# The Hyena projection inside the first MLP stage of a two-layer diffusion backbone

## The chip, the cores and the metric

The kernel runs on one core of one Trainium2 chip. The metric is the device time of the core in microseconds, as the median over several executions. The engines are TensorE (PE; its weight loads are PEld), VectorE (DVE), ScalarE (ACT), GpSimd (POOL) and SyncE (SP), which in this kernel only issues DMAs.

## The reference

A stream of 1024 latent tokens and one of 256 context tokens, each of width 1024, pass through two layers. Every sub-layer is: RMS norm, shift and scale by the conditioning, the sub-layer, RMS norm, gate, residual. Layer 0 mixes by attention, layer 1 by a Hyena long convolution beside a Mamba-2 scan; both end with a squared-ReLU MLP of hidden width 4096. What matters for the change, cut from the reference:

```python
x = x + mx[5] * rms_norm(sq_relu_mlp(modulate(rms_norm(x, g[2]), mx[3], mx[4]), ff_w1[i], ff_w2[i]), g[3])   # layer 0; ctx likewise
hx = modulate(rms_norm(x, g[0]), mx[0], mx[1])          # layer 1
px = hx @ w_in
hy_x, z_x, m_x = split_cols(px, (ODD_HY, ODD_Z, ODD_XBC + ODD_DT))   # 1536, 512, 1024 + 16 columns
uc = centred_dwconv(hy_x, short_w, short_b)             # 3 taps along the tokens, latent tokens only
m_c = (hc @ w_in[:, ODD_CTX_START:])                    # context tokens: only mamba's columns

z = concatenate([t, cos(ph), -sin(ph)])                 # 33 position features of 1024 positions
h = sin(fr * (z @ w1 + b1))                             # 64 hidden units
h = sin(fr * (h @ w2 + b2))
h = (h @ w3) * decay                                    # the long filters, further on
```

## The kernel before

Features lie on the 128 partitions, tokens along the free axis. The 1280 tokens are worked in three chunks (`CHUNKS`): latent 0 to 511, latent 512 to 1023, and the 256 context tokens. Each float32 product is three products of rounded parts: high by high, high by low and low by high. So every weight piece of 128 x 1024 (512 KB) is fetched by SP, rounded by ACT (`w_high`) and split by DVE (`w_low`, raw less high) before PE uses it; the activations lie likewise as `h_high` and `h_low`. Every engine's instructions are written out in a fixed order, semaphores tie them together, and each function below is a stage: it ends with a barrier of all engines, and its memory and semaphores are new.

`out_and_mlp` (L1181) runs twice, once at the end of each layer. Its work is a list of `steps`, one weight piece each: 24 of the output projection, then for each chunk eight rounds of four pieces up (L1397) and four down (L1414), 216 steps in layer 0. In step i, ACT first rounds piece i+2 and DVE splits piece i+2, SP fetches piece i+3, PE multiplies piece i, and DVE adds the down products to the residual tile (`mixed`, L1602). Six PSUM banks go round. Beside the steps, a table of step numbers (`gate_at`, `square_x_at`, `scale_at` and others, filled in the loop over the six jobs q) places each chunk's closing norm: squares on ACT (L1453), their sum on POOL (L1614), the column sum by an all-ones matmul (L1366), reciprocal root on ACT (L1457, L1459), gating and residual on DVE (L1542, L1551), then the same again for layer 1's opening norm (L1495, L1633, L1372), scale (L1560), shift and rounding (L1503) and splitting (L1535). For the first chunks this lies beside the steps of the next chunk. The last job, q = 5, is the context chunk's; it has no steps left beside it, and the stage runs on without products until `END`.

`project_hyena` (L2293) is the next stage. A `WeightRing` (L334) does fetch, rounding and splitting with two slots; twelve pieces give two units of 512 tokens each, 24 matmuls a unit (L370). ACT copies them to `hy_raw` (L2361), DVE convolves with three operations (L2415 to L2419), SP stores each result to `scratch_hyena`. Beside it the feature network runs: its two small products on PE (L2339), the angle and its reduction to less than half a turn in seven DVE operations a layer (L2377 to L2391), the sine on ACT (L2365), and at the end seven small reversed or shifted copies of the result (`flip`, L2396 to L2403).

`project_mamba` (L1638) follows. It fetches the step-size weights and multiplies them (L1681), then eight xbc pieces of three units each, whose convolution (L1779 to L1783) and SiLU (L1666) lie beside the products, and last four z pieces, two units of 512 each, whose SiLU is the gate (L1737). On DVE only two splits lie beside the z products. The next stage, `scan_states`, opens with 60 transposes on PE (L1823) that ACT copies out (L1831).

## Time and profile before

| | |
|---|---|
| median of three runs | 3692.05 us (3689.9 to 3698.3) |
| profiled execution | 3690.47 us |
| its span | 3688.5 us |
| PE busy | 3471.0 us, 94% |
| DVE, ACT, POOL busy | 1830.5, 1332.2, 690.2 us |
| mean DMA rate | 111 GB/s |

The span runs from the first to the last instruction of the profiled execution; some 2 us lie around it. PE's busy time counts pipelined matmuls whose modelled durations overlap, so the distance from one start to the next says more than the duration. The granted clock (PEclk) has two levels here, 1.00 for 2.4 GHz and 0.50 for 1.2 GHz; a figure between them is a window in which it changed. A line such as L370 is a helper's, shared by several stages, so the place in time has to be given with it.

### The profile page before, as it was taken

To read this page: it belongs to the slowest core of one execution; us is meant where nothing else is said; L and a number is where in the kernel's file an instruction comes from. 1 tells how busy PE (TensorE), PEld (TensorE's weight loads), DVE (VectorE), ACT (ScalarE), POOL (GpSimd) and SP (SyncE) were. 2 spreads that over 40 slices of the span, in tenths; PEclk is the share of its full clock that TensorE was granted. 3 is DMA by queue.
4 is the path that set the end of the run, shared out by engine and by line. 5 is a ranking of instruction groups with operands and counts; after the bars stand their busy time and mean duration, and the time that the engine had idled before them with its cause. 6 is when DMAs were issued, how large, how long until landed. Compare 5 with 4: busy or idle time off the path is not lost. (4 is left out here: it accounts for less than half of the span.)

```text
span 3688.5 us, 40136 instructions
## 1 busy us (share of the span) xinstructions
PE 3471.0 (94%) x15670; PEld 2471.0 (67%) x15670; DVE 1830.5 (50%) x2317; ACT 1332.2 (36%) x2143; POOL 690.2 (19%) x398
## 2 busy tenths in 40 slices
PE   6989799999899999999996989899989899999997
PEld 3655244555688888888886868653344688888886
DVE  3332744433266554554675534476355565444444
ACT  4323344444554333333453223441110443223332
POOL 0000277666332201200211000110000230002001
PEclk8999799999999999999998999998999999999999
DMA  8744532321244333433453211101501343333332
GB/s 336 277 165 122 146 68 58 79 56 45 92 149 136 116 97 97 137 97 97 155 190 126 92 53 40 36 35 58 199 18 52 114 166 97 97 97 120 120 97 97
DMA packets 140528, 408.65 MB, mean 111 GB/s; under 512 B 24621, under 2 KB 41421, under 8 KB 136052
## 3 DMA queue, kind: packets, MB, share of 16 engines
q1 hardware_dynamic: 140340, 406.08, 33.8%
q8 instruction: 125, 2.05, 0.2%
q14 instruction: 63, 0.52, 0.0%
HBM read 344.73 MB, written 61.21 MB: 110 GB/s over the span
## 5 line engine op out<-in xcount | busy, mean ns | idle before, releaser
L1438 ACT ACTIVATE w_high<-w_raw 128x1024 fp32r<-128x1024 f32 x360 | 380.1, 1056 | 579.8 <-PE psum L1414 471.9
L1524 DVE TENSOR_TENSOR w_low<-w_raw,w_high 128x1024 fp32r<-128x1024 f32 x360 | 453.2, 1259 | 119.8 <-ACT w_high L1438 118.8
L1414 PE MATMUL psum<-hid_high,w_high 128*128 128x512 f32 (+1 forms) x1280 | 472.6, 369 | 10.3 <-DVE hid_low L1592 8.7
L1397 PE MATMUL psum<-h_high,w_high 128*128 128x512 f32 (+1 forms) x1280 | 474.7, 371 | 2.1 <-DVE w_low L1524 2.1
L1397 PE MATMUL psum<-h_high,w_low 128*128 128x512 f32 (+1 forms) x1280 | 470.9, 368 | 0.0
L1397 PE MATMUL psum<-h_low,w_high 128*128 128x512 f32 (+1 forms) x1280 | 470.9, 368 | 0.0
L1414 PE MATMUL psum<-hid_low,w_high 128*128 128x512 f32 (+1 forms) x1280 | 470.8, 368 | 0.0
L1414 PE MATMUL psum<-hid_high,w_low 128*128 128x512 f32 (+1 forms) x1280 | 470.8, 368 | 0.0
L1614 POOL TENSOR_TENSOR squares_then_rstd_of_out<-squares_then_rstd_of_out,square_out 128x512 f32<-128x512 f32 (+1 forms) x70 | 102.4, 1464 | 1284.7 <-ACT square_out L1453 1284.1
L1178 POOL TENSOR_TENSOR probs_added<-probs_added,probs_turned 128x1024 f32<-128x1024 f32 x128 | 305.0, 2383 | 66.7 <-ACT probs_turned L1107 62.5
L1146 DVE TENSOR_REDUCE row_max<-psum 128x1 f32<-128x1280 f32 x128 | 190.3, 1491 | 243.6 <-PE psum L1055 147.3
L1589 DVE TENSOR_TENSOR hid_high<-hid_relu 128x512 fp32r<-128x512 f32 (+1 forms) x160 | 113.8, 711 | 350.2 <-ACT hid_relu L1514 350.0
L1107 ACT ACTIVATE probs_turned<-psum 128x512 f32<-128x512 f32 (+1 forms) x352 | 193.5, 577 | 251.5 <-PE psum L1017 249.8
L1414 PEld LDWEIGHTS psum<-hid_high,w_high 128*128 128x128 f32 x1280 | 241.2, 188 | 53.0 <-DVE hid_low L1592 5.8
L370 PE MATMUL psum<-h_high,w_high 128*128 128x512 f32 (+1 forms) x664 | 252.3, 380 | 24.1 <-DVE w_low L363 24.1
L1397 PEld LDWEIGHTS psum<-h_high,w_high 128*128 128x128 f32 x1280 | 241.3, 189 | 44.7 <-DVE w_low L1524 2.7
L1397 PEld LDWEIGHTS psum<-h_low,w_high 128*128 128x128 f32 x1280 | 241.3, 189 | 41.6 <-issue 1.9
L1414 PEld LDWEIGHTS psum<-hid_low,w_high 128*128 128x128 f32 x1280 | 241.3, 188 | 40.1 <-issue 0.2
L1397 PEld LDWEIGHTS psum<-h_high,w_low 128*128 128x128 f32 x1280 | 241.3, 189 | 39.9
L1414 PEld LDWEIGHTS psum<-hid_high,w_low 128*128 128x128 f32 x1280 | 241.3, 189 | 39.8
L370 PE MATMUL psum<-h_low,w_high 128*128 128x512 f32 (+1 forms) x664 | 245.7, 370 | 0.0
L370 PE MATMUL psum<-h_high,w_low 128*128 128x512 f32 (+1 forms) x664 | 245.6, 370 | 0.0
(406 smaller groups left out, 5385.8 us busy)
## 6 DMA issues: line engine op xcount, KB each, us to landing
w_raw<-in_ff_w_dram SPq DMA_DIRECT2D x320, 512.0 KB, 3.5
ada_ring<-in_ada_w_dram SPq DMA_DIRECT2D x24, 2048.0 KB, 9.5
w_raw<-in_w_out_dram SPq DMA_DIRECT2D x40, 512.0 KB, 3.5
stream_in<-scratch_x SPq DMA_DIRECT2D x32, 256.0 KB, 4.0
scratch_spectra<-spectrum_out SPq DMA_DIRECT2D x32, 256.0 KB, 2.0
filter_ring<-scratch_spectra SPq DMA_DIRECT2D x16, 512.0 KB, 4.8
w_raw<-in_w_hy_dram SPq DMA_DIRECT2D x12, 512.0 KB, 3.5
scratch_hyena<-hy_conv SPq DMA_DIRECT2D x12, 512.0 KB
```

The costliest lines, as they stand in the source:

```text
L370: mm = pe.matmul(out, x[:, k, :], y[:, k, a:a + n], start=(k == 0 and i == 0), stop=(k == KT - 1 and i == 2))
L1107: act.activation(pt[:, i % RING, h, 0:nq], g.ps[:, T_BANK + h, 0:nq], ACT.Exp).then_inc(exped, 1)
L1146: dve.tensor_reduce(neg_max[:, u % 2, 4 * h + t:4 * h + t + 1], area[:, 0:TOK], AX.X, ALU.max, negate=True).then_inc(maxed, 1)
L1178: pool.tensor_tensor(total, old, pt[:, i % RING, :, 0:nq], ALU.add).then_inc(added, 1)
L1397: mm = pe.matmul(bank[:, 0:n], x[:, i % SLOTS, k, :], y[:, k, a:a + n], start=(k == 0 and m == 0), stop=(k == KT - 1 and m == 2))
L1414: mm = pe.matmul(bank[:, 0:n], x[:, i % SLOTS, 2 * k + half, :], y[:, k, 0:n], start=(k == 0 and m == 0), stop=(k == HT - 1 and m == 2))
L1438: act.activation(w_hi[:, i % SLOTS], raw[:, i % 2], ACT.Copy).then_inc(w_rounded, 1)
L1524: dve.tensor_tensor(w_lo[:, i % SLOTS], raw[:, i % 2], w_hi[:, i % SLOTS], ALU.subtract).then_inc(w_split, 1)
L1589: dve.tensor_tensor(hid_hi[:, j, 0:n], relu[:, v % 2, 0:n], relu[:, v % 2, 0:n], ALU.mult).then_inc(hid_rounded, 1)
L1614: pool.tensor_tensor(acc_out[:, q % 2, 0:n], acc_out[:, q % 2, 0:n], sq_out[:, v % 2, 0:n], ALU.add).then_inc(added_out, 1)
```

## The change

`project_hyena` is gone. Its twelve weight pieces are steps 216 to 227 of `out_and_mlp` in layer 0 (kind "next"), with that stage's three weight slots and six banks, and the convolution takes its place in DVE's step. The raw products lie in the tile of the MLP's ReLU and square, the results in two rows of the residual tile, from where they are stored. The last job's norm is placed beside these steps, two feature rows a step for gate and residual, four a step for scaling. The convolution no longer pads: it starts with the middle tap over all 1024 tokens and adds the outer two over 1023. The feature network moves into `project_mamba`: its products follow z units 1 and 5, its DVE operations the splits beside z tiles 1 and 3, its sines the gates of units 3 and 7, and `flip` is DVE's last work there. It borrows the raw and accumulator tiles of mamba's convolution, so the positions are fetched once the seventh convolution is done.

```diff
-def out_and_mlp(nc, g, src, w_out, w_ff, x_from, x_mid, x_to, layer, norm_to, tokens):
+def out_and_mlp(nc, g, src, w_out, w_ff, x_from, x_mid, x_to, layer, norm_to, tokens, w_next=None, next_to=None):
...
+    NEXT, LAST = 12 if norm_to else 0, len(steps)
+    steps = steps + [(None, "next", t) for t in range(NEXT)]
...
+    beside_next = [NEXT > 0 and q == JOBS - 1 for q in range(JOBS)]
...
         def beat(k):
-            return k // 2 if q == 0 else wide * k
+            return k // 2 if q == 0 or beside_next[q] else wide * k
...
-                at = begin + (k // 4 if q == 0 else wide * k)
+                at = begin + (k // 4 if q == 0 or beside_next[q] else wide * k)
...
-    END = max(list(split_at) + list(store_at)) + 1
+    END = max(max(list(split_at) + list(store_at)) + 1, N + 1)
...
+        next_raw = hidden[:].rearrange("p h n -> p (h n)").rearrange("p (s n) -> p s n", s=2)
+        next_res = out[:, 0:2, 0:LAT]
...
+                    t = i - LAST - 1
+                    if 0 <= t < NEXT:
+                        sp.wait_ge(convolved, t + 1)
+                        sp.dma_start(next_to[:, t, :], next_res[:, t % 2, :]).then_inc(next_stored[t % 2], 16)
...
+                def next_units(i):
+                    for half in range(2):
+                        a, n = spans[half]
+                        bank = bank_for(unit_of[i, half])
+                        for k in range(KT):
+                            if i == LAST:
+                                pe.wait_ge(split, KT * (C + half) + k + 1)
+                            for m, (x, y) in enumerate(((w_hi, high), (w_hi, low), (w_lo, high))):
+                                mm = pe.matmul(bank[:, 0:n], x[:, i % SLOTS, k, :], y[:, k, a:a + n], start=(k == 0 and m == 0), stop=(k == KT - 1 and m == 2))
+                        mm.then_inc(product, 1)
...
-                    if i >= N or kind(i) == "down":
+                    if i >= N or kind(i) in ("down", "next"):
                         spread_sums(i)
...
+                    elif i < N and c is None:
+                        for half in range(2):
+                            u, (a, n) = unit_of[i, half], spans[half]
+                            act.wait_ge(product, u + 1)
+                            if j >= 2:
+                                act.wait_ge(convolved, j - 1)
+                            act.activation(next_raw[:, j % 2, a:a + n], g.ps[:, u % BANKS, 0:n], ACT.Copy).then_inc(next_out, 1)
...
+                def convolve(t):
+                    x, y = next_raw[:, t % 2, :], next_res[:, t % 2, :]
+                    tap = lambda i: vec(g, "short_w", i * NEXT + t)
+                    dve.wait_ge(next_out, 2 * (t + 1))
+                    if t >= 2:
+                        dve.wait_ge(next_stored[t % 2], 16 * (t // 2))
+                    if t == 0:
+                        dve.wait_ge(x_stored[0], 16 * (C + 2))
+                    dve.tensor_scalar(y, x, tap(1), vec(g, "short_b", t), ALU.mult, ALU.add).then_inc(stepped, 1)
+                    dve.wait_ge(stepped, 2 * t + 1)
+                    dve.scalar_tensor_tensor(out=y[:, 1:LAT], in0=x[:, 0:LAT - 1], scalar=tap(0), in1=y[:, 1:LAT], op0=ALU.mult, op1=ALU.add).then_inc(stepped, 1)
+                    dve.wait_ge(stepped, 2 * t + 2)
+                    dve.scalar_tensor_tensor(out=y[:, 0:LAT - 1], in0=x[:, 1:LAT], scalar=tap(2), in1=y[:, 0:LAT - 1], op0=ALU.mult, op1=ALU.add).then_inc(convolved, 1)
...
-def project_mamba(nc, g, d, high, low, xbc, gate, dt, adt):
+def project_mamba(nc, g, d, high, low, xbc, gate, dt, adt, f):
...
+        zt, turns, ang, h1 = raw[:, 0, 0:LAT], raw[:, 1, 0:LAT], acc[:, 0, 0:LAT], acc[:, 1, 0:LAT]
...
+                    if t == TILES:
+                        sp.wait_ge(conv, TILES - 1)
+                        sp.dma_start(zt[0:33], d["positions"]).then_inc(positions_in, 16)
...
+                    if u in (1, 5):
+                        layer = u // 4
+                        pe.wait_ge(loaded, 32)
+                        pe.wait_ge(positions_in, 16)
+                        if layer:
+                            pe.wait_ge(sines, 1)
...
+                    if u in (3, 7):
+                        layer = u // 4
+                        act.wait_ge(reduced, 6 * (layer + 1))
+                        act.activation((h1[rows], h2[rows, 0:LAT])[layer], ang[rows], ACT.Sin).then_inc(sines, 1)
...
-                for t in range(TILES, TILES + Z_TILES):
-                    ring.split_piece(dve, t + 1)
+                for t in range(Z_TILES):
+                    ring.split_piece(dve, TILES + t + 1)
+                    if t % 2 == 1:
+                        layer = t // 2
+                        if layer == 0:
+                            dve.wait_ge(conv_read, 2 * TILES)
+                            dve.wait_ge(conv, TILES)
+                        angle(layer)
+                        whole_turns(layer)
+                        for j in range(3):
+                            take_off(layer, j)
+                        clamp(layer)
+                flip()
...
-            project_hyena(nc, g, d, g.high, g.low, sc.u3, f)
```

The functions `angle`, `whole_turns`, `take_off`, `clamp` and `flip` are those of `project_hyena`, word for word, on the borrowed tiles.

The orders below show three places. First PE at the end of the context chunk, before the change: the last down products, the two column sums of the last norm, the branches of the stage border, and the first Hyena product.

```order
L1414 MATMUL psum<-hid_high,w_low 128x256
L1366 MATMUL psum<-squares_then_rstd_of_out,all_ones 128x256
L1372 MATMUL psum<-squares_then_rstd_of_x,all_ones 128x256
L1305 UNCONDITIONAL_BRANCH
L2331 UNCONDITIONAL_BRANCH
L370 MATMUL psum<-h_high,w_high 128x512
```

PE at the first column sum after the change, at the border of steps 216 and 217; L1443 is a Hyena product and L1383 the column sum.

```order
L1443 MATMUL psum<-h_high,w_high 128x512
L1443 MATMUL psum<-h_low,w_high 128x512
L1443 MATMUL psum<-h_high,w_low 128x512
L1383 MATMUL psum<-squares_then_rstd_of_out,all_ones 128x256
L1443 MATMUL psum<-h_high,w_high 128x512
```

The column sum stood between the MLP's last product and the stage border; now 48 Hyena products stand ahead of it, and the border stands behind all of them.

Then DVE at the same place, before: the last split of a weight piece (L1524), the additions of the last down products, and the norm's gating and residual.

```order
L1524 TENSOR_TENSOR w_low<-w_raw,w_high 128x1024
L1602 TENSOR_TENSOR mixed<-mixed,psum 128x256 x6
L1542 SCALAR_TENSOR_TENSOR mixed<-mixed,modulation,psum 128x256
L1551 TENSOR_TENSOR mixed<-mixed,stream_in 128x256
```

DVE after the change, from the additions of step 214 to those of step 218's norm; L1561 splits a piece, L1655 adds down products, L1608 to L1612 are a convolution, L1579 and L1588 gate and residual.

```order
L1561 TENSOR_TENSOR w_low<-w_raw,w_high 128x1024
L1655 TENSOR_TENSOR mixed<-mixed,psum 128x256 x2
L1561 TENSOR_TENSOR w_low<-w_raw,w_high 128x1024
L1655 TENSOR_TENSOR mixed<-mixed,psum 128x256 x2
L1561 TENSOR_TENSOR w_low<-w_raw,w_high 128x1024
L1608 TENSOR_SCALAR mixed<-hid_relu_and_square,small_vectors 128x1024
L1610 SCALAR_TENSOR_TENSOR mixed<-hid_relu_and_square,small_vectors,mixed 128x1023
L1612 SCALAR_TENSOR_TENSOR mixed<-hid_relu_and_square,small_vectors,mixed 128x1023
L1561 TENSOR_TENSOR w_low<-w_raw,w_high 128x1024
```

A split now stands ahead of each pair of additions and ahead of each convolution, always of the piece two steps on.

Last ACT at the end of mamba's projection, before: the last rounding (L357), the last gates (L1737), the branches, and the first copy of the scan stage.

```order
L357 ACTIVATE w_high<-w_raw 128x1024
L1737 ACTIVATE gate<-psum 128x512 x4
L1663 UNCONDITIONAL_BRANCH
L1826 UNCONDITIONAL_BRANCH
L1831 ACTIVATE x_tokens<-psum 128x512
```

ACT there after the change; L1811 is the gate and L1815 a sine, the first into the borrowed accumulator, the second into the result tile.

```order
L1811 ACTIVATE gate<-psum 128x512 x2
L1815 ACTIVATE conv_acc<-conv_acc 64x1024
L357 ACTIVATE w_high<-w_raw 128x1024
L1811 ACTIVATE gate<-psum 128x512 x4
L1815 ACTIVATE hy_h_19524<-conv_acc 64x1024
L1721 UNCONDITIONAL_BRANCH
L1953 UNCONDITIONAL_BRANCH
```

The first sine stands ahead of the last rounding, the second behind the last gate, and no table load stands between them.

## Rows read from the trace of the kernel before

**Rows 1.** The page, part 1: busy time, share of the span, instructions.

```profile
PE 3471.0 (94%) x15670; PEld 2471.0 (67%) x15670; DVE 1830.5 (50%) x2317; ACT 1332.2 (36%) x2143; POOL 690.2 (19%) x398
```

**Rows 2.** Windows: length, busy of PE, PEld, DVE, ACT, POOL, PEclk, DMA share, GB/s.

```profile
1985.90:2015.30 29.40, 2.27 (x5) 0.82 (x4) 17.20 (x37) 11.38 (x23) 7.10 (x9) 0.53 0.30 99
2015.30:2151.90 136.60, 136.54 (x584) 109.96 (x584) 64.29 (x65) 26.75 (x38) 0.00 (x0) 0.99 0.23 81
```

**Rows 3.** Waits, 1985 to 2016 and, last row, 1800 to 1987: total us, times, longest.

```profile
PE psum L370 <- DVE w_low L363: 14.6, 1, 14.6
...
PE psum L1397 <- DVE w_low L1524: 2.1, 2, 1.4
```

**Rows 4.** Timeline of PE: start us, us, what, and idle time before.

```profile
1985.63 0.28 PE L1414 MATMUL psum<-hid_high,w_low 128*128 128x256 f32 x1
...
2015.31 0.80 PE L370 MATMUL psum<-h_high,w_high 128*128 128x512 f32 x1 [14.64 <-DVE w_low L363]
...
2151.47 0.39 PE L370 MATMUL psum<-h_high,w_low 128*128 128x512 f32 x1
2163.99 0.61 PE L1681 MATMUL psum<-h_high,w_dt_high 128*16 128x512 f32 x1 [12.14 <-DVE w_dt_low L1742]
```

**Rows 5.** Timeline of DVE; page, parts 5 and 6.

```profile
1976.87 1.22 DVE L1524 TENSOR_TENSOR w_low<-w_raw,w_high 128x1024 fp32r<-128x1024 f32 x1 [0.63 <-ACT w_high L1438]
...
L1438 ACT ACTIVATE w_high<-w_raw 128x1024 fp32r<-128x1024 f32 x360 | 380.1, 1056 | 579.8 <-PE psum L1414 471.9
...
w_raw<-in_ff_w_dram SPq DMA_DIRECT2D x320, 512.0 KB, 3.5
```

**Rows 6.** The chain that ended last, in order of time: start us, us.

```profile
3600.87 21.76 PE psum L1414 x96
```

**Rows 7.** Groups of 2012 to 2156: count, busy us, mean ns, idle before (layer 1).

```profile
L2339 PE MATMUL psum<-positions,hy_w 33*64 33x512 f32 x4 | 1.9, 602 | 0.0
```

**Rows 8.** Windows of 2 us at three places, columns as in rows 2.

```profile
2154.00:2156.00 2.00, 0.00 (x0) 0.00 (x0) 1.94 (x2) 0.00 (x0) 0.00 (x0) 0.79 0.00 0
2168.00:2170.00 2.00, 2.00 (x9) 0.76 (x7) 1.57 (x1) 0.00 (x0) 0.00 (x0) 0.80 0.71 244
2346.00:2348.00 2.00, 0.23 (x1) 0.23 (x2) 1.72 (x2) 1.98 (x8) 1.57 (x2) 0.58 0.51 156
```

**Rows 9.** The same chain, at a column sum of the second MLP stage.

```profile
2924.51 0.86 PE psum L1366 x2
```

**Rows 10.** Timeline of DVE, then groups of 2012 to 2156.

```profile
2008.08 0.48 DVE L1535 SCALAR_TENSOR_TENSOR h_low<-norm_scaled,modulation,h_high 128x256 fp32r<-128x256 f32 x1 [0.18 <-ACT h_high L1503]
...
L2419 DVE SCALAR_TENSOR_TENSOR hy_conv<-hy_raw,small_vectors,hy_conv 128x1024 f32<-128x1024 f32 x12 | 15.4, 1285 | 0.4
...
L2415 DVE TENSOR_SCALAR hy_conv<-hy_raw,small_vectors 128x1024 f32<-128x1024 f32 x12 | 9.8, 814 | 71.6 <-ACT hy_raw L2361 71.6
```

**Rows 11.** Groups of 2012 to 2156, then timeline of DVE: features and copies.

```profile
L2387 DVE SCALAR_TENSOR_TENSOR angles<-turns,angles 64x1024 f32<-64x1024 f32 x6 | 7.3, 1212 | 0.1
L2377 DVE TENSOR_SCALAR angles<-psum,small_vectors 64x1024 f32<-64x1024 f32 x2 | 2.7, 1332 | 0.0
L2365 ACT ACTIVATE hy_h<-angles 64x1024 f32<-64x1024 f32 x2 | 2.1, 1056 | 0.0
...
L2381 DVE TENSOR_SCALAR turns<-angles 64x1024 f32<-64x1024 f32 x2 | 1.4, 686 | 0.1
...
L2365 ACT ACT_TABLE_LOAD x1 | 1.3, 1283 | 0.0
...
2145.02 0.28 DVE L2396 COPY hy_h_flipped<-hy_h 64x256 f32<-64x256 f32 x1
...
2145.94 0.14 DVE L2403 COPY hy_h_sines<-hy_h 64x1 f32<-64x1 f32 x1
```

**Rows 12.** Timeline of ACT and PE at the end of mamba's projection.

```profile
2335.00 0.60 ACT L1737 ACTIVATE gate<-psum 128x512 f32<-128x512 f32 x1 [4.84 <-PE psum L370]
...
2336.39 7.55 PE L1823 MATMUL psum<-identity,xbc 128*128 128x128 f32 x60 [1.42 <-PEq L92]
```

More of the change, by code:

```diff
@@ L1194, in out_and_mlp @@
     steps = [(c, None, t) for c in range(C) for t in range(KT)] + [(c, e, j) for c in range(C) for e in range(EIGHTHS) for j in range(PIECES)]
+    NEXT, LAST = 12 if norm_to else 0, len(steps)
+    steps = steps + [(None, "next", t) for t in range(NEXT)]
     N = len(steps)
-    units = [(i, half) for i, (c, e, j) in enumerate(steps) for half in range(1 if e is None or j < HT else 2)]
+    units = [(i, half) for i, (c, e, j) in enumerate(steps) for half in range(1 if e is None or (c is not None and j < HT) else 2)]
     unit_of = {x: u for u, x in enumerate(units)}
@@ L1201, in kind @@
         c, e, j = steps[i]
-        return "out" if e is None else "up" if j < HT else "down"
-    released = {"out": 0, "up": 0, "down": 0}
+        return "next" if c is None else "out" if e is None else "up" if j < HT else "down"
+    released = {"out": 0, "up": 0, "down": 0, "next": 0}
     release = []
@@ L1355, in bank_for @@
                             pe.wait_ge(up_free, count)
+                        elif what == "next":
+                            pe.wait_ge(next_out, count)
                         else:
@@ L1420, in _ @@
                         pe.wait_ge(w_split, i + 1)
-                        if kind(i) == "out":
+                        if kind(i) == "next":
+                            next_units(i)
+                        elif kind(i) == "out":
                             out_unit(i)
@@ L1585, in _ @@
                     split_weights(i + 2)
-                    if i < N and e is not None and j < HT:
+                    if i < N and c is None:
+                        convolve(j)
+                    elif i < N and e is not None and j < HT:
                         v = (c * EIGHTHS + e) * HT + j
@@ L1633, in _ @@
                             pool.tensor_tensor(acc_x[:, 0:m], acc_x[:, 0:m], sq_x[:, v % 2, 0:m], ALU.add).then_inc(added_x, 1)
-                    if i < N and steps[i][1] is None:
+                    if i < N and kind(i) == "out":
                         add_square_of_out(steps[i][0], steps[i][2])
-def project_mamba(nc, g, d, high, low, xbc, gate, dt, adt):
+def project_mamba(nc, g, d, high, low, xbc, gate, dt, adt, f):
     TILES, Z_TILES, BANKS = 8, 4, 4
@@ L1700, in _ @@
                     ring.product_of(pe, g.ps[:, 4 + u % 2, 0:n], TILES + t, high, low, a, n).then_inc(product, 1)
+                    if u in (1, 5):
[4 more added lines that the diff above has]
+                            pe.wait_ge(sines, 1)
+                        w, src, kk = ((w1, zt, 33), (w2, h1, HID))[layer]
+                        for c in range(2):
+                            mm = pe.matmul(g.ps[rows, 6 + c, :], w[0:kk, :], src[0:kk, c * BANK:(c + 1) * BANK], start=True, stop=True)
+                        mm.then_inc(feature_product, 1)
             @block.scalar
@@ L1783, in _, with angle @@
                     dve.scalar_tensor_tensor(out=out, in0=raw[:, t % 2, 2:2 + n], scalar=tap(2), in1=out, op0=ALU.mult, op1=ALU.add).then_inc(conv, 1)
-                for t in range(TILES, TILES + Z_TILES):
-                    ring.split_piece(dve, t + 1)
+                a, k = ang[rows], turns[rows]
+                def angle(layer):
+                    dve.wait_ge(feature_product, layer + 1)
+                    if layer:
+                        dve.wait_ge(sines, 1)
+                    flat = g.ps[rows, 6:8, :].rearrange("p b n -> p (b n)")
+                    b = vec(g, ("hy_b1", "hy_b2")[layer])[rows, :]
+                    dve.tensor_scalar(a, flat, b, vec(g, "freq")[rows, :], ALU.add, ALU.mult).then_inc(biased, 1)
@@ L2748, in layer_1 @@
                 dt, adt = tile(nc, steps, "dt", [P, KTILES, 16], "right"), tile(nc, steps, "adt", [P, KTILES, 16], "right")
-                project_mamba(nc, g, d, g.high, g.low, xbc, f.gate, dt, adt)
+                project_mamba(nc, g, d, g.high, g.low, xbc, f.gate, dt, adt, f)
                 g.parts_memory.close()
```

186 lines of the change are left out of this document (47 added, 139 removed).

## The prediction

> **What bounds the kernel now.** I read the page first, then the windows by stage, the waits between the stages, and the timelines of TensorE (PE), ScalarE (ACT) and VectorE (DVE) at the stage borders. PE is busy 94% of the span [rows 1], so a change pays where PE stands still, or where its matmuls run at half clock. Two windows are the place of the change [rows 2]: 29.4 us with 2.3 us of PE work and a granted clock of 0.53 (the last chunk's norm and the opening of the Hyena projection), then 136.6 us of solid PE work (the projection). Behind them PE stands for 12.3 us until mamba starts [rows 4]. The wait that ends the first window last is that of the first Hyena matmul for its weights' low half, 14.6 us [rows 3]. These could not be fetched before the norm was done, because they belong to the next stage.
>
> **Hyena as weight steps 216 to 227.** The last MLP matmul starts at 1985.63 us and would be followed 0.12 later; the first Hyena matmul starts at 2015.31 [rows 4]. If its weights are ready, it now starts at 1985.75: 29.56 saved. The inputs of the two latent chunks are long split; the last chunk (256 context columns) isn't read by Hyena.
>
> Are the weights ready? Step 216's raw piece can be fetched when piece 214 is split, at 1976.87 + 1.22 = 1978.09; landing takes 3.5 us, rounding 1.06 and splitting 1.22 [rows 5], so it could be split at 1983.9. In DVE's row it stands ahead of step 214's additions, in ACT's ahead of step 214's squares; queued behind step 213's work it may be 1984.4. PE needs it at 1985.75. I count no wait; if the split is late as two of the last chunks' are (2.1 us in two waits, the longest 1.4) [rows 3], it costs up to 1.4. Behind the waiting split stand only two additions of the last chunk, whose banks PE doesn't need for two steps.
>
> The 576 matmuls cost the same: 96 of the same shape take 21.76 us [rows 6], 0.2267 each, so 130.56 for the projection and 10.88 for a step. Before they took 2015.31 to 2151.70 (the last start plus 0.23), 136.39. The 5.8 over are the feature network's products, 1.9 us for the first layer [rows 7] and the same for the second, so 3.8, and 2.0 of half clock at the start, since PE came out of the window at 0.53. Out of full-clock work that 2.0 goes too.
>
> **The last chunk's norm beside it.** Its additions, squares and scalings come off the path, but its two column sums on PE now stand between Hyena's matmuls. In the second MLP stage such a sum over 512 columns takes 0.86 of PE's chain [rows 9]; at 256 columns I take half, 0.45 each, 0.9 in all (bounds 0 and 1.7). The chain of the norm, from the last MLP product at 1985.75 to its last split at 2008.08 + 0.48, 22.8 us, has steps 216 to 226 for it. DVE's fullest step is 225: eight operations of 0.48 us, one split of 1.22 and one convolution of 0.81 + 1.28 + 1.28 [rows 10], 8.4 of 10.88. The split for two steps later stands ahead of the convolution that must wait for PE, so PE isn't held. SP's row gets, between weight fetches, the eight stream tiles, two stores of the norm and the twelve of Hyena; each of its waits is for work of the step before, and a fetch stands three steps ahead of its use. I take nothing for it.
>
> **The end of the stage.** As before, ACT's last copy, the convolution, the last store and its landing, the barrier, and mamba's own fetch follow the last matmul, so the 12.3 us from 2151.70 to 2163.99 [rows 4] and the cold start of mamba stay. Dropping a stage border is in the 29.56 already.
>
> **The features beside mamba's z products.** The 3.8 us of PE move, they don't go: minus 3.8 in Hyena, plus 3.8 here. Positions are fetched once convolution 6 is done, two tiles ahead of use. Between z products of 5.44 us: after tile 0 the features take 1.9 on PE; rounding and splitting piece 10 keep DVE until 2.3; then angles 1.33, three operations of 0.69 and three of 1.21 [rows 11], with gaps 7.2, until 9.5 (the other two groups of 0.69, the whole turns' second half and the clamp, read as the one shown). The sine waits for unit 3's gate, at 10.9 + 1.9 + 0.6 = 13.4, so it never waits for DVE, and piece 11, rounded 1.06 later than before, is still needed only 10 us on. But the second sine now stands behind the last gate, and the seven small copies behind it. Before, the last gate ran 2335.00 to 2335.60 and PE began the next stage at 2336.39 [rows 12]. Now the sine adds 1.06 less 0.1 of overlap, and the copies 1.06 (2145.02 to 2146.08) [rows 11]: plus 2.05. PE is then idle for 3.5 us instead of 1.42. After Hyena's end the clock fell within 3.3 us (still 0.79 in the window from 2154, where 0.50 is the lower level, 1.2 GHz); after the scan's transposes, which ended at 2336.39 + 7.55 = 2343.94, within 2.4 (0.58 in the window from 2346) [rows 8, 12]. So I expect the transposes to start at half clock. It came back about 4.8 us after work began at 2163.99 (0.80 in the window from 2168), which loses half of that, 2.4; Hyena's own cold start lost the 2.0 above. If the clock holds, nothing. I take 2.0.
>
> One rule speaks against this part. The first sine before is preceded by a table load of 1.28 us [rows 11], and in ACT's row of the changed kernel no load stands between a gate and a sine. The Trainium skill (ScalarE: Activation LUTs, Rules for kernel authors) says to budget about 2.7 us for every switch to a different table set. If the gate's function and the sine were of different sets, the tail would hold one load more, and the estimate by the page would be 23.8 saved instead of 26.5. The trace's 1.28 decides against the page's size, and the row without a load against a switch at all.
>
> **Sum.** -29.56 (gap) - 2.0 (cold start) + 0.9 (column sums) + 2.05 (tail) + 2.0 (cold scan) = -26.6. The profiled execution took 3690.47 us (span 3688.5 and 2.0 around it); this gives 3663.9. The median of the three runs is 1.6 higher, so 3665.5 by it. I forecast 3664.5.
>
> **Rivals.**
> *Smaller gain.* PE waits somewhere in the new steps: the late first piece (1.4), a late piece or bank in some steps, a feature product that holds the z products, or a clock whose falls in the scan come out otherwise. For: the two late splits [rows 3] show that fetch, round and split in turn barely keep up at 2.9 us a step (24 matmuls of 0.12). Against: new steps are 10.88 long. With 4 to 12 us lost: about 3668 to 3676, middle 3672.
> *The gap only moves.* If the norm chain ends behind Hyena's last product instead of beside it, 22.8 come back at the stage's end: 3687. It decides at the last split of the chunk's norm: in step 226 of 227 by the order, behind step 228 for this rival. For: beats are now steps four times as long, and the last scalings stand two steps from the end. Against: 11 us a step.
> *Slower.* If a weight piece were split only behind the convolution of the step before its use, each step would be 10.88 of products, then copy 0.6, convolution 3.4, split 1.2 in line: 5.2 for each of 11 steps, 57 us, 3664.5 + 57 = 3721, slower than before from 2.4 us of wait a step. Place: DVE's row in the new steps. Against: split i+2 stands ahead of convolution i. Stores that hold the two result slots would do the same (copy, convolution and store are 0.6 + 3.4 + the 3.5 of a fetch as the nearest row, 7.5 of the 21.8 us that a slot has).
>
> **How the numbers follow.** Forecast 0.84, smaller gain 0.10, the moved gap 0.03, slower 0.03. No change is within 0.2%, 7 us, which is about what a measurement of this kernel can tell. The forecast and the smaller gain are faster (0.94), the moved gap is within (0.03), the last slower (0.03). The low end 3657: the scan's clock falls cost nothing or less (-2), piece and sums nothing (-1), runs and clock phase 4. The high end 3674 takes in most of the smaller gains.
>
> **What would show it.** Right: PE's start-to-start gap at the end of the last chunk below 1.5 us, granted clock 1.00 through it; Hyena's products 131.5 us from first to last; the norm's last split before the last Hyena product; the same 12.3 us to mamba; the second sine right behind the last gate without a table load; 3.5 us of PE idle ahead of the transposes, and a window at 0.50 behind. Wrong: PE waits for a split or a bank in Hyena's steps, for positions or a sine among the z products, a stage end longer than 12.3 us, or a clock below 1.00 in the now unbroken stretch.

## The result, and the profile after

The changed kernel takes 3663.54 us (median, 3660.55 to 3665.49) against 3692.2 (3689.9 to 3698.3) for the kernel before, a ratio of 0.9921, 95% interval [0.9906, 0.9936]. It is faster by 28.7 us. Its profiled execution took 3665.49 us (before 3690.47), its span is 3663.7. That execution is the slowest of the four timed, and the profiled one of before lies below its median, so the two profiles compared here differ by less, 24.75 us of span.

The page, part 1, against [rows 1]: outside its modelled busy time PE has 182 us of the span, before 217.5.

```profile
PE 3481.7 (95%) x15670; PEld 2476.7 (68%) x15670; DVE 1825.2 (50%) x2316; ACT 1328.2 (36%) x2142; POOL 700.6 (19%) x398
```

The timeline of PE where the gap of [rows 4] was, at the end of the Hyena products, and at the end of mamba's (start us, us, what, idle before). L1431 is the last MLP product, L1443 Hyena's, L1745 mamba's step sizes, L370 its z products, L1950 the scan's transposes.

```profile
1985.04 0.28 PE L1431 MATMUL psum<-hid_high,w_low 128*128 128x256 f32 x1
1985.16 0.40 PE L1443 MATMUL psum<-h_high,w_high 128*128 128x512 f32 x1
...
2116.49 0.39 PE L1443 MATMUL psum<-h_high,w_low 128*128 128x512 f32 x1
2127.33 0.61 PE L1745 MATMUL psum<-h_high,w_dt_high 128*16 128x512 f32 x1 [10.45 <-DVE w_dt_low L1820]
...
2301.38 0.39 PE L370 MATMUL psum<-h_high,w_low 128*128 128x512 f32 x1
2305.29 8.74 PE L1950 MATMUL psum<-identity,xbc 128*128 128x128 f32 x60 [3.52 <-PEq L92]
```

The first Hyena product follows the last MLP product after 0.12 us instead of 29.68, at 0.40 us instead of 0.80. In PE's waits from 1985 to 2305 us the stage border is all that is left (total us, times, longest), where [rows 3] had 14.6 for a weight:

```profile
PE psum L1745 <- DVE w_dt_low L1820: 10.4, 1, 10.4
```

DVE shows why nothing waits: step 216's piece is split at 1982.65 + 1.22, 1.3 us ahead of its use, and the norm's last two splits run in step 226, ahead of Hyena's last product.

```profile
1982.65 1.22 DVE L1561 TENSOR_TENSOR w_low<-w_raw,w_high 128x1024 fp32r<-128x1024 f32 x1 [1.10 <-ACT w_high L1468]
...
2099.16 0.88 DVE L1572 SCALAR_TENSOR_TENSOR h_low<-norm_scaled,modulation,h_high 128x256 fp32r<-128x256 f32 x2
```

The windows of the joined stretch, of the border behind it and of the scan's start, columns as in [rows 2]. The one of 0.53 is gone; the clock falls at the border and in the tail.

```profile
1985.10:2116.80 131.70, 131.70 (x582) 108.77 (x581) 65.49 (x78) 32.47 (x57) 14.11 (x11) 1.00 0.29 100
2116.80:2127.30 10.50, 0.08 (x1) 0.00 (x0) 3.67 (x4) 2.19 (x3) 0.00 (x0) 0.67 0.22 75
2304.00:2306.00 2.00, 0.71 (x4) 0.74 (x5) 0.40 (x4) 0.00 (x0) 0.00 (x0) 0.69 0.00 0
2306.00:2308.00 2.00, 2.00 (x11) 2.00 (x10) 0.00 (x0) 1.18 (x3) 0.00 (x0) 0.50 0.28 66
2308.00:2310.00 2.00, 2.00 (x19) 1.91 (x17) 0.00 (x0) 1.90 (x6) 0.00 (x0) 0.95 0.00 0
```

ACT and DVE in the tail, answering to [rows 11, 12]: the sine (L1815) overlaps the last gate (L1811) by 0.1 us with no table load between them, and the seven copies follow, the last of them L1896.

```profile
2301.80 0.60 ACT L1811 ACTIVATE gate<-psum 128x512 f32<-128x512 f32 x1 [4.84 <-PE psum L370]
2302.30 1.04 ACT L1815 ACTIVATE hy_h<-conv_acc 64x1024 f32<-64x1024 f32 x1
...
2303.37 0.28 DVE L1889 COPY hy_h_flipped<-hy_h 64x256 f32<-64x256 f32 x1 [5.42 <-ACT hy_h L1815]
...
2304.30 0.14 DVE L1896 COPY hy_h_sines<-hy_h 64x1 f32<-64x1 f32 x1
```

The whole difference, from the start of one kind of PE work to that of the next, in us. Each kernel has three profiles: the two compared here and four of the experiments below. "Change" is that of the first two. "Transforms" is counted from the first product with `dft_odd` behind the filter taps, "folded" to the first such product of the folded signal; "opening" is from the first product with `adt` to the first with `segments`.

| stretch on PE | before | after | forecast | change |
|---|---|---|---|---|
| last MLP product to first of Hyena | 29.68, 29.27, 29.25 | 0.12, 0.12, 0.12 | -29.56 | -29.56 |
| Hyena, first to last | 136.15, 137.17, 136.20 | 131.33, 131.33, 131.33 | -4.9 | -4.82 |
| last of Hyena to first of mamba | 12.53, 10.52, 11.86 | 10.84, 10.70, 10.71 | 0 | -1.69 |
| mamba, first to last | 170.58, 170.39, 170.90 | 174.05, 173.96, 174.72 | +3.8 | +3.47 |
| last z product to first transpose | 1.81, 1.81, 1.81 | 3.91, 3.91, 3.91 | +2.05 | +2.10 |
| transposes, to the next matmul behind | 11.39, 11.39, 11.41 | 12.57, 12.52, 12.72 | +2.0 | +1.18 |
| opening of the scan | 24.36, 24.29, 24.52 | 21.20, 21.18, 21.53 | 0 | -3.16 |
| Hyena's filter taps, to the transforms | 46.56, 46.52, 46.63 | 52.16, 52.16, 52.12 | 0 | +5.60 |
| transforms, to the folded ones | 138.35, 137.69, 138.39 | 141.35, 141.36, 137.71 | 0 | +3.00 |

All else differs by 0.9 us in sum (2.8 more ahead of the MLP's products, 3.4 less within them, 0.3 less elsewhere), and the rows add up to -23.9: -24.75 with it, the difference of the spans. In the forecast's five rows and the border it is -29.3; the last three rows give 5.4 back.

### The profile page after: what moved, and what is told of

Same layout as the page of the kernel before. It is cut to its first block and busy times, and to the rows that moved or that the text cites. A ratio compares the mean times of both kernels' runs of the same rounds, so it can differ in the third digit from the quotient of the medians.

```text
span 3663.7 us, 40128 instructions
## 1 busy us (share of the span) xinstructions
PE 3481.7 (95%) x15670; PEld 2476.7 (68%) x15670; DVE 1825.2 (50%) x2316; ACT 1328.2 (36%) x2142; POOL 700.6 (19%) x398
## 3 DMA queue, kind: packets, MB, share of 16 engines
q8 instruction: 125, 2.05, 0.2%
## 5 line engine op out<-in xcount | busy, mean ns | idle before, releaser
L1468 ACT ACTIVATE w_high<-w_raw 128x1024 fp32r<-128x1024 f32 x372 | 392.5, 1055 | 576.3 <-PE psum L1431 472.1
L1561 DVE TENSOR_TENSOR w_low<-w_raw,w_high 128x1024 fp32r<-128x1024 f32 x372 | 466.4, 1254 | 122.1 <-ACT w_high L1468 121.3
L1431 PE MATMUL psum<-hid_high,w_high 128*128 128x512 f32 (+1 forms) x1280 | 472.4, 369 | 8.7 <-DVE hid_low L1645 7.4
L1414 PE MATMUL psum<-h_high,w_high 128*128 128x512 f32 (+1 forms) x1280 | 474.8, 371 | 0.3 <-DVE w_low L1561 0.2
L1414 PE MATMUL psum<-h_high,w_low 128*128 128x512 f32 (+1 forms) x1280 | 470.9, 368 | 0.0
L1414 PE MATMUL psum<-h_low,w_high 128*128 128x512 f32 (+1 forms) x1280 | 470.9, 368 | 0.0
L1431 PE MATMUL psum<-hid_low,w_high 128*128 128x512 f32 (+1 forms) x1280 | 470.8, 368 | 0.0
L1431 PE MATMUL psum<-hid_high,w_low 128*128 128x512 f32 (+1 forms) x1280 | 470.8, 368 | 0.0
L1642 DVE TENSOR_TENSOR hid_high<-hid_relu_and_square 128x512 fp32r<-128x512 f32 (+1 forms) x160 | 113.7, 710 | 350.4 <-ACT hid_relu_and_square L1551 350.3
L1431 PEld LDWEIGHTS psum<-hid_high,w_high 128*128 128x128 f32 x1280 | 241.3, 188 | 50.8 <-DVE hid_low L1645 6.4
L1431 PEld LDWEIGHTS psum<-hid_low,w_high 128*128 128x128 f32 x1280 | 241.3, 189 | 40.1 <-issue 0.2
L1431 PEld LDWEIGHTS psum<-hid_high,w_low 128*128 128x128 f32 x1280 | 241.3, 189 | 40.0
L1551 ACT ACTIVATE hid_relu_and_square<-psum 128x512 f32<-128x512 f32 (+1 forms) x160 | 88.5, 553 | 412.2 <-PE psum L1414 412.1
L370 PE MATMUL psum<-h_high,w_high 128*128 128x512 f32 (+1 forms) x472 | 176.8, 375 | 9.4 <-DVE w_low L363 9.4
L1027 PE MATMUL psum<-probs_turned,v_pair 128*64 128x512 f32 (+1 forms) x704 | 183.7, 601 | 0.8 <-ACT attended L1114 0.8
```

What stands on the lines that cost most here:

```text
L370: mm = pe.matmul(out, x[:, k, :], y[:, k, a:a + n], start=(k == 0 and i == 0), stop=(k == KT - 1 and i == 2))
L1027: mm = pe.matmul(g.ps[64 * h:64 * h + 64, V_BANK, 0:nq], v[:, pair % 2, kt, h, :], pt[:, i % RING, h, 0:nq], start=(kt == lo), stop=(kt == ...
L1414: mm = pe.matmul(bank[:, 0:n], x[:, i % SLOTS, k, :], y[:, k, a:a + n], start=(k == 0 and m == 0), stop=(k == KT - 1 and m == 2))
L1431: mm = pe.matmul(bank[:, 0:n], x[:, i % SLOTS, 2 * k + half, :], y[:, k, 0:n], start=(k == 0 and m == 0), stop=(k == HT - 1 and m == 2))
L1468: act.activation(w_hi[:, i % SLOTS], raw[:, i % 2], ACT.Copy).then_inc(w_rounded, 1)
L1551: act.activation(relu[:, v % 2, 0:n], g.ps[:, u % BANKS, 0:n], ACT.Relu).then_inc(up_free, 1)
```

## The experiments

**The changed kernel twice more.** No edit. The second time it ran beside the warm version at the end.

> The changed kernel as it is, once more. Theory: the local terms are fixed by the order of the work and repeat to 0.2 us (0.12 us between the last MLP product and the first Hyena product, 131.3 us from first to last Hyena product, 3.9 us from the last z product to the first transpose); the stretches that the edits don't touch (the 46.5 us against 52.2 us from the first feature product of the spectra to its first transform, the 1.7 us less before mamba's first product) are chance of clock and DMA, and will come out differently by some us here. Rival: these stretches are a lasting effect of the change, and come out as in the first trace (52.2 us, 10.8 us). Ratio to before 0.992 +- 0.001 by both.

> The changed kernel as it is, beside the next run on the same chip, for a direct comparison. Both theories: Hyena's products 131.3 from first to last start, 10.7 to mamba's first product, 174.0 from it to the last z product, 3.9 to the first transpose, 12.5 for the transposes; some 3663 us. The place of sparse stretches is left open: if chance sets their clock, the stretch of the spectra is 46.5 or 52.2 us long, and may come out otherwise than in the two profiles of this kernel so far (52.2 both); if the change sets it, 52.2 a third time.

Measured: 3662.84 us (3659.35 to 3671.12), ratio 0.9914 [0.9897, 0.9931]; and 3668.14 (3659.69 to 3674.34), 0.9935 [0.9921, 0.9949]. By stretches see the table: from the last MLP product to the transposes the three profiles agree within 0.8 us a row, while the fold differs by 3.6 between them. The first expectation's theory, that the untouched stretches would come out otherwise, failed: its rival's 52.2 for the filter taps and 10.8 ahead of mamba came again, and 52.1 a third time.

**The kernel before twice more.** No edit.

> The kernel before, profiled once more, nothing edited. After four kernels with the features in mamba all gave 10.7 us instead of 12.5 before mamba's first product, 21.2 instead of 24.4 us from the scan's first column product to its segments, and 52.1 instead of 46.6 us to the spectra's transform, either these are states that a run falls into (theory: clock level and DMA landing; this trace shows some of the later values) or they belong to the features' place (rival: it shows 12.5, 24.4 and 46.6 again).

> The kernel before with nothing edited, a third profile. If PE's history sets the clock of the sparse stretches, 24.3 us for the scan's opening and 46.5 for the spectra, as in the two so far; if chance does, 21.2 and 52.2 are as likely. Hyena's gap 29.3 to 29.7 and its first product at half clock either way; the pause ahead of mamba 10.5 to 12.5, by the landing of its step-size weights.

Measured: 3691.14 and 3690.79 us. The pause ahead of mamba is 10.52 and 11.86 us with nothing changed, so the -1.69 of that row can come without the change: ACT waited 2.51, 0.49 and 1.82 us for the step-size weights in the three profiles of before, and 0.64 in the changed kernel's. That the change has no part in it isn't shown, since in all eleven profiles with the features in mamba this wait is 0.47 to 0.64. The scan's opening and the filter taps take 24.3 to 24.5 and 46.5 to 46.6 in all three.

**The features alone.** The kernel before, with only the feature network moved into `project_mamba`, by the diff's own lines.

```diff
-def project_mamba(nc, g, d, high, low, xbc, gate, dt, adt):
+def project_mamba(nc, g, d, high, low, xbc, gate, dt, adt, f):
...
+                    if u in (1, 5):
+                        layer = u // 4
+                        pe.wait_ge(loaded, 32)
+                        pe.wait_ge(positions_in, 16)
```

> One part alone: the kernel before, with its own Hyena stage, but the feature network moved beside mamba's z products. Theory: Hyena's products get 3.8 us shorter, mamba's 3.7 us longer, the tail behind the last gate 2.1 us longer and the transposes 1.2 us: 3.3 us slower than before, about 3695.5, ratio 1.0009, within what can be told from no change. Rival (the tail is hidden, or costs the clock more): 3692 with a first transpose that starts no later, or 3700 and more with half clock through the scan.

Measured: 3694.08 us (3689.41 to 3707.49), ratio 1.0006 [0.9994, 1.0018]: this half of the change gains nothing. Hyena's products take 133.38 us (2.8 less than before), mamba's 175.11, the tail 3.91, the transposes 12.72. The gap stays at 29.21. Since 575 distances of 0.2267 are 130.35, what is left of Hyena's 133.38 is 3.0 of half clock at the start. These 2.8 us aren't what the feature products cost, because that start differs from profile to profile: 14 distances are 0.43 or more here, 7 in the profile of before, 12 and 7 in its repeats, which is 3.0, 1.7, 2.7 and 1.7 us. The features' own cost is read in the profile of before at the first layer (L2339), between the Hyena product ahead of it and the one behind:

```profile
2027.63 0.39 PE L370 MATMUL psum<-h_high,w_low 128*128 128x512 f32 x1
2027.94 1.93 PE L2339 MATMUL psum<-positions,hy_w 33*64 33x512 f32 x4
2029.80 0.50 PE L370 MATMUL psum<-h_high,w_high 128*128 128x512 f32 x1
```

The distance is 2.17 instead of 0.23, and the next one 0.34, so a layer costs 2.06 us and both cost 4.1. Among mamba's z products it is the same 2.06 a layer (2264.58 to 2266.75 and 0.34 in the changed kernel).

**The features earlier among the z products.** The second sine then stands ahead of the last gates.

```diff
-                    if u in (1, 5):
-                        layer = u // 4
+                    if u in (0, 3):
+                        layer = (0, 3).index(u)
...
-                    if u in (3, 7):
-                        layer = u // 4
+                    if u in (2, 5):
+                        layer = (2, 5).index(u)
...
-                    if t % 2 == 1:
+                    if t in (0, 2):
```

> The changed kernel with the features one step earlier beside the z products: feature products after units 0 and 3 instead of 1 and 5, sines after the gates of units 2 and 5 instead of 3 and 7. Theory (the tail is the second sine and the seven copies behind the last gate, and the cold transposes follow from the longer pause): the pause from the last z product to the first transpose falls from 3.9 to 1.8 us, the transposes with their copies from 9.6 to 8.4 us, together 3.3 us less, time about 3660. Rival (the DVE chain of 7.2 us doesn't fit, so that PE waits for a split or a sine among the z products): waits of 1 us and more on PE there, z products longer than 4 x 10.88 + 3.8, nothing gained.

Measured: 3666.36 us (3659.7 to 3667.77), ratio 0.9916 [0.9899, 0.9934]. PE's timeline at the last z product and the transposes:

```profile
2306.29 0.39 PE L370 MATMUL psum<-h_high,w_low 128*128 128x512 f32 x1
2308.16 7.55 PE L1950 MATMUL psum<-identity,xbc 128*128 128x128 f32 x60 [1.48 <-PEq L92]
```

The distance is 1.87 again (3.91), and the transposes run 7.55 instead of 8.74: both terms of the tail are the second sine's place, 3.2 us together. The whole time doesn't show it: 3660 was expected, and the median is 3.5 above the repeated changed kernel's in the same comparison. Against the repeated changed kernel's profile this one is 5.6 us longer before the first Hyena product, where nothing was edited: 3.0 ahead of the MLP's first down product and 2.6 from there to its last, a stretch that takes 875.8 to 882.0 us over all profiles.

**The norm at its old pace.** The last chunk's norm takes two steps a beat, as the other chunks' do.

```diff
-    beside_next = [NEXT > 0 and q == JOBS - 1 for q in range(JOBS)]
+    beside_next = [False for q in range(JOBS)]
```

> The changed kernel without the dense placement of the context chunk's norm: one row a step for gate, residual and scaling, as for the other chunks, so that the scalings stand in steps 228 to 235, behind the last Hyena product. Theory (the dense placement only matters for what it keeps out of the stage's end): scale, shift and split of eight rows, 0.8 us each, 6.5 us, start when the last convolution is done (4 us after the last product) and end about 10.8 us after it, where the last store lands at about 7.4: 3.4 us slower than the changed kernel, about 3667. Rival (the whole gap comes back): over 20 us, 3685 and more; or nothing, since the store's landing covers it: 3663.5.

Measured: 3671.26 us (3662.71 to 3678.26), ratio 0.9933 [0.9914, 0.9952]. Hyena's products take 130.85 us (one column sum less among them, so 0.48 each), and the border 14.74 instead of 10.7. DVE, behind the last convolution, scales and splits the norm's last rows before the stage can end:

```profile
2118.26 1.28 DVE L1612 SCALAR_TENSOR_TENSOR mixed<-hid_relu_and_square,small_vectors,mixed 128x1023 f32<-128x1023 f32 x1
2119.46 0.87 DVE L1597 SCALAR_TENSOR_TENSOR norm_scaled<-mixed,modulation,psum 128x256 f32<-128x256 f32 x2
...
2125.90 0.48 DVE L1572 SCALAR_TENSOR_TENSOR h_low<-norm_scaled,modulation,h_high 128x256 fp32r<-128x256 f32 x1 [0.18 <-ACT h_high L1533]
```

So by the profile the table of beats is worth 3.6 us (3.4 was expected), and the rival of the moved gap is shown in small: what of the norm stands behind the last product costs its time. The median is 8.4 above the repeated changed kernel's in the same comparison; its six times spread over 15.6 us, and what the rest is isn't shown.

**The weights split late.** In the Hyena steps the piece of the next step is split behind the convolution, which is the slower rival of the prediction.

```diff
-                    split_weights(i + 2)
+                    if i + 2 <= LAST or not NEXT:
+                        split_weights(i + 2)
...
+                        split_weights(i + 1)
```

> The changed kernel with each Hyena piece after the first split behind the convolution of the step before it, instead of two steps ahead of its use. Theory (the order of DVE's row is what keeps the steps at 10.88 us): a product step, then copy 0.6, convolution 3.4 and split 1.2 in line, 16.1 us a step for eleven steps, Hyena's first to last product 131.3 + 57 = 188 us, the whole about 3720, slower than before. Rival (PE's queue of banks and slots absorbs it, or the three weight slots do): 3664 to 3670.

Measured: 3749.07 us, ratio 1.0155 [1.0142, 1.0169]: slower than the kernel before. Hyena's products take 216.39 us, 85 more. The waits, then DVE and PE at the border of the first two steps, and windows of the same place:

```profile
PE psum L1443 <- DVE w_low L1561: 57.6, 11, 5.3
```

```profile
2000.90 0.81 DVE L1608 TENSOR_SCALAR mixed<-hid_relu_and_square,small_vectors 128x1024 f32<-128x1024 f32 x1 [11.12 <-ACT hid_relu_and_square L1545]
...
2004.27 1.22 DVE L1561 TENSOR_TENSOR w_low<-w_raw,w_high 128x1024 fp32r<-128x1024 f32 x1
```

```profile
2005.55 0.78 PE L1443 MATMUL psum<-h_high,w_high 128*128 128x512 f32 x1 [4.88 <-DVE w_low L1561]
```

```profile
1998.90:2004.20 5.30, 1.76 (x8) 1.13 (x6) 3.23 (x3) 0.60 (x1) 0.00 (x0) 1.00 0.00 0
2004.20:2009.00 4.80, 3.46 (x8) 2.81 (x9) 1.29 (x2) 0.07 (x1) 0.00 (x0) 0.64 0.32 109
```

The rival's wait was priced right: 57.6 us in 11 waits against 57. Its time was not. Another 27.5 us, 2.5 a step in the mean, is the clock, which falls in every pause, so that the first products behind, 8 in some steps and 13 or 14 in the others, start 0.43 apart instead of 0.23. The Trainium skill (TensorE: Matmul & The Clock Gate, HAM oscillation — how this bites in real kernels) describes this of a kernel that waits for a DMA in every tile and pays the fall in every tile. The trace agrees, here with a wait for a split: all eleven steps behind a pause begin with such products.

**The tail filled.** 14 products into a free bank stand behind the last z product, to keep the clock up for the transposes. They add work that the result doesn't use.

```diff
+                pe.wait_ge(raw_out, U)
+                for r in range(14):
+                    pe.matmul(g.ps[:, 0, :], ring.high[:, 1, r % KT, :], high[:, r % KT, 0:BANK], start=True, stop=True)
```

> The changed kernel with 14 products of 128x512 that nobody reads behind the last z product, while the second sine and the copies run; the rest is unchanged. Theory (the 1.2 us that the transposes lose is the half clock after the pause): the last real z product to the first transpose stays 3.9 us, the transposes with their copies come back from 12.5 to 11.4 us, 1.2 less, not to be told in the whole time. Rival (the transposes are slow for their first copies' sake, or the triangles' fetch): 12.5 as before.

> The changed kernel with 14 products into a free bank behind the last z product, once more, to see whether the clock of the sparse stretches behind mamba belongs to the program or to chance. So far the scan's opening takes 24.4 us and the spectra 46.6 in both profiles of the kernel before and in the one of this kernel; it takes 21.2 and 52.2 in all nine others with the features in mamba. If PE's own history ahead of the stretch sets it, this run shows 24.4 and 46.6 again. If chance does, 21.2 and 52.2 are the likelier, as in nine of ten.

Measured: 3663.58 us (3651.81 to 3666.98), ratio 0.9916 [0.9901, 0.9931], and 3662.83 for the single run later.

```profile
2298.92 3.33 PE L1777 MATMUL psum<-h_high,w_high 128*128 128x512 f32 x14
2303.09 7.56 PE L1953 MATMUL psum<-identity,xbc 128*128 128x128 f32 x60 [0.83 <-PEq L92]
```

The transposes take 7.56 us again, so their 1.2 are the clock's, but the distance from the last z product is 4.40 instead of 3.91: the products themselves hold the border up by 0.5. The first profile has 24.38 for the scan's opening and 46.57 for the filter taps, as before has. The second, of the same program, has 21.83 and 52.11, as the changed kernel has.

**Early features and a warm border.** On top of the early features, 30 such products stand behind Hyena's last and 12, then 8, ahead of mamba's first.

```diff
+                    if NEXT and i == N - 1:
+                        for r in range(30):
+                            pe.matmul(bank_for(len(units)), w_hi[:, 0, r % KT, :], high[:, r % KT, 0:BANK], start=True, stop=True)
...
+                for r in range(8):
+                    pe.matmul(g.ps[:, 0, :], high[:, r % KT, 0:P], high[:, r % KT, 0:BANK], start=True, stop=True)
```

> The early features of the second run, and products that nobody reads across the border between the MLP stage and mamba: 30 of 128x512 behind the last Hyena product and 12 ahead of mamba's first. Theory (the pause of 10.7 us drops the clock, and mamba starts at half of it): granted clock 1.00 across the border, step-size products back to back at 0.23 us, 2.2 us less from mamba's first product to its last, the pause itself unchanged; about 3658, the fastest of these kernels. Rival (the fillers delay the barrier or the first product, or the clock falls all the same): pause longer than 10.9 us, 174.0 us of mamba products again.

> The changed kernel with the feature products behind z units 0 and 3 and their sines at the gates of units 2 and 5, 30 products into a free bank behind the last Hyena product, and 8 (not 12) ahead of mamba's first step-size product, so that these end when its weights are ready. Theory: pause between Hyena's last product and mamba's first 10.7 again (11.12 with 12), products of mamba 172.5, tail 1.87, transposes 11.39: 5.1 less than the changed kernel in these places, so 3658 if it stands at 3663. Rival, that such pauses at half clock cost nothing that the sum sees: the same time as the changed kernel, within 2 us, as was seen for the early features alone.

Measured: 3657.4 us (3653.2 to 3665.12), ratio 0.9911 [0.9896, 0.9926], with 12; 3662.89 (3653.69 to 3668.49), 0.992 [0.9906, 0.9933], with 8. PE at the border in the version with 8:

```profile
2118.21 0.39 PE L1443 MATMUL psum<-h_high,w_low 128*128 128x512 f32 x1
2118.44 6.96 PE L1461 MATMUL psum<-h_high,w_high 128*128 128x512 f32 x30
2126.49 2.06 PE L1745 MATMUL psum<-h_high 128*128 128x512 f32 x8 [1.09 <-PEq L92]
2128.93 0.40 PE L1750 MATMUL psum<-h_high,w_dt_high 128*16 128x512 f32 x1 [0.38 <-DVE w_dt_low L1825]
```

The border takes 10.72 us from Hyena's last product (11.12 with 12), mamba's products 172.56, the tail 1.87, the transposes 11.39: 5.5 us less in these places than the changed kernel in the same comparison (202.06 to 196.54). The two medians stand 5.25 apart, the same way and size, though the intervals of their ratios overlap. Over all calls the two warm versions have a mean of 3660.7 us (12 runs), the changed kernel 3664.8 (16 runs), each with a standard deviation of 4.5 to 5.0, though the runs come from several comparisons. So the warm version is likely better by some 4 us, near the limit of what these runs can tell.

## Why the prediction was right

The forecast was 3664.5 us and the median is 3663.5; faster had 0.94. That the two lie 1.0 apart is in part luck: repeats of one kernel have medians up to 5.3 us apart, and misses of up to 5.6 us in single rows partly cancel. What the profiles bear out is the mechanism of the large terms. By the steps of the prediction:

- *The gap.* -29.56 forecast and measured. No wait for step 216's weights: split at 1983.87 and needed at 1985.16. The MLP ends 0.59 us earlier in this profile, so the match with the 1983.9 to 1984.4 worked out says little; the slack is 1.3 us, where 1.35 to 1.85 was worked out.
- *Hyena's products.* First to last 131.33 us, against "131.5". The total of -4.9 held, its parts did not quite: the 5.8 over are 4.1 for the feature products and 1.7 for the cold start, where 3.8 and 2.0 were counted. The feature products' busy time of 1.9 is less than the 2.06 by which a layer puts off the products behind it. The cold start is no fixed term: 1.7 to 2.7 us in three profiles of the kernel before. The column sums cost 0.98 for two (131.33 less 130.35), against 0.9.
- *The norm beside them.* No wait of PE in the new steps, the last split in step 226 as the order said. The norm at its old pace shows that the place matters.
- *The border.* Unchanged as a mechanism. Its 12.3 us (12.5 from start to start) were one of several values: 10.5 to 12.5 in three profiles of one kernel.
- *The features.* +3.5 against +3.8, again with parts that cancel: the products cost 4.1, and mamba's start lost 0.7 less to the clock than in the profile of before (its first 72 distances take 15.38 us against 16.09). The prediction kept that start unchanged; against 13.85 in the warm version it cost 1.4 to 2.6 us over the profiles. The sine waits for its gate alone.
- *The tail.* +2.10 against +2.05. The rule of the Trainium skill (ScalarE: Activation LUTs, Rules for kernel authors) that was weighed as 2.7 us more has no case here, since gate and sine follow without a load. (26.6 less 2.7 is 23.9; the prediction's 26.5 and 23.8 are rounded otherwise.)
- *The cold transposes.* The mechanism was right and the size off: 1.2 instead of 2.0, as both the early features and the filled tail show. The clock was back some 3 us after the first transpose, not 4.8 (0.95 in the window from 2308). Until then 13 transposes start 0.21 apart where they start 0.11 apart in the profile of before, about 1.3 us, and the 60 together take 8.74 against 7.55 us.

What the prediction did not see is the pair of sparse stretches behind mamba. Here they are in the profile before, the changed kernel's, and the filled tail's second profile (the filter taps; in the first two the scan's opening too):

```profile
2476.60:2523.10 46.50, 36.78 (x58) 12.79 (x59) 36.82 (x56) 2.45 (x3) 0.00 (x0) 0.67 0.17 68
2347.80:2372.10 24.30, 19.94 (x46) 11.04 (x46) 17.67 (x23) 13.57 (x27) 6.39 (x4) 0.68 0.33 121
```

```profile
2443.50:2495.60 52.10, 46.77 (x58) 16.45 (x59) 36.80 (x56) 2.47 (x3) 0.00 (x0) 0.54 0.15 61
2317.80:2339.00 21.20, 16.62 (x46) 8.99 (x46) 17.05 (x23) 13.64 (x27) 6.20 (x4) 0.84 0.37 137
```

```profile
2438.00:2490.00 52.00, 44.23 (x88) 16.97 (x87) 36.84 (x56) 1.28 (x1) 0.00 (x0) 0.57 0.15 61
```

The instructions are the same, the granted clock isn't, and the sum of the two is 70.8 to 71.2 us in one form and 73.3 to 74.0 in the other. The first theory was plain chance. It doesn't stand as it is: all three profiles of before have the one form, and ten of eleven with the features in mamba have the other. That the place of the features alone sets it doesn't stand either, since one program, the filled tail's, showed both. What is shown: the form can change without an edit, and the kernel with its features in mamba shows the dearer one nearly always. What sets it stays open; in the changed kernel's three profiles the pair takes 2.5 us more in the mean. By the means of three profiles each, the six stretches up to the scan gain 28.4 us and this pair gives 2.5 back, 25.9, beside the 26.6 forecast. The fold's 3.0 in the first comparison can come without an edit: from the last transform product to the first folded one it is 35.5, 35.5 and 31.9 us in the three profiles of the changed kernel (31.8 to 32.5 in those of before).

## What to carry to other kernels

Where a stage ends in a chain that PE doesn't take part in, take the next stage's products as further steps of it: the gain is the gap as the timeline shows it, and the clock that PE keeps comes on top. Read from the order whether each weight split still stands ahead of the work that waits for PE; one split a step behind it cost 85 us, more than the whole change brought. Price a repeated pause as the wait and the clock's fall behind it, and a moved piece of work by what it then stands behind (here a sine behind the last gate, 3.2 us in the profile), not by its own length. And before a row's difference is split into causes, read the first products behind the pause in each profile: a cold start that varies by 1 us looks like a gain or a loss of the edit.

## What the runs showed of the hardware

- A PE pause of 5.2 us in the mean in each of eleven steps cost 7.7: 2.5 more for products at half clock behind it.
- Of 60 transposes at the start of a stage, the fall to 1.2 GHz cost 1.1 to 1.4 us, of 128x512 products 1.4 to 3.0 us; the cost differs by about 1 us between executions of one kernel.
- A stretch with sparse PE work takes 46.5 or 52.1 us with the same instructions, by the clock it is granted.
- The step-size weights' landing held ACT for 0.49 to 2.51 us in three executions of the kernel before, and the border took 10.5 to 12.5 us with it.
- Gate and sine ran back to back without a table load; the load of 1.28 us that stood ahead of the first sine in Hyena's stage is gone now that a gate stands there (15 loads in the profile instead of 16).
- Four feature products of 1.93 us busy between 128x512 products cost 2.06 us of PE's time from start to start.
